# Two layers of hybrid attention on one core: where the steps of the layer normalisation stand among the matrix products

## The reference

```python
for l in range(DEPTH):
    need_ctx = l < DEPTH - 1
    shift, scale, gate = jnp.split(cond @ w_ada[l] + b_ada[l], 3, axis=-1)
    h = x * (1.0 + scale[:, None]) + shift[:, None]
    ...
    x = layer_norm(ALPHA * x + gate[:, None] * y, ln_g[l], ln_b[l])
    if need_ctx:
        cx = layer_norm(ALPHA * cx + gate_c * yc, ln_g[l], ln_b[l])
return x
```

## Time and profile before

| | |
|---|---|
| median of three runs | 1734.81 us |
| the profiled execution, own time | 1734.62 us |
| its span, first to last instruction | 1732.7 us |
| TensorE busy | 94% of the span |
| VectorE busy | 39% |
| ScalarE busy | 32% |
| mean granted TensorE clock | 0.976 of full |
| layer 0's chunk 3 out products end, layer 1's begin | about 973 us |
| layer 1's chunk 2 out products begin | about 1647 us |

### The profile page before, as it was taken

How to read it: one execution, slowest core, us unless ns; L and a number is a source line. 1 busy time by engine, 2 the same in 40 slices (tenths; PEclk the granted TensorE clock), 3 DMA queues, 4 the chain that set the end, 5 groups by cost and what they waited for, 6 DMA issues and landing times.

```text
span 1732.7 us, 25988 instructions
## 1 busy us (share of the span) xinstructions
PE 1624.4 (94%) x10106; PEld 1028.6 (59%) x10106; DVE 671.8 (39%) x1529; ACT 549.1 (32%) x1256; POOL 36.8 (2%) x108
## 2 busy tenths in 40 slices
PE   6999999899999999889999899999899799999996
PEld 4666866556565556544747665675564355555484
DVE  2123444413323214321255624244445265554165
ACT  0232242323323224432022332124214365554023
POOL 0000000000000000000000000000000011111000
PEclk9999999899999999999999998999999899999997
DMA  9100021112123113000545411000001000001353
GB/s 382 55 25 25 1 98 62 61 61 105 43 73 122 50 37 123 25 13 28 183 144 164 161 49 49 13 25 26 13 1 49 25 13 1 25 14 43 107 174 115
DMA packets 41144, 120.63 MB, mean 70 GB/s; under 512 B 4288, under 2 KB 14784, under 8 KB 39744
## 3 DMA queue, kind: packets, MB, share of 16 engines
q1 hardware_dynamic: 41024, 118.97, 19.6%
HBM read 109.52 MB, written 9.44 MB: 69 GB/s over the span
## 4 chain that ended last, share of the span: by engine, by line
PE 72%; issue 16%; DVE 6%; ACT 3%; DMA 1%; POOL 0%; SPq 0%; DVEq 0%; ACTq 0%; POOLq 0%
PE proj L986 22%; PE mixed L986 12%; PE scores L986 5%; PE proj L970 4%; PE mixed L970 3%; PE mixed L1106 3%; PE turned L1092 3%; PE scores L1204 2%; PE scores L1072 2%; PE scores L1232 2%; PE scores L1075 1%; ACT vstage L1669 1%; PE turned L1243 1%; PE mixed L931 1%; ACT yT L1669 1%
## 5 line engine op out<-in xcount | busy, mean ns | idle before, releaser
L986 PE MATMUL proj<-hT,weights 128*128 128x512 f32 (+1 forms) x1280 | 519.5, 552 | 10.3 <-DVE yT L1354 3.6
L986 PEld LDWEIGHTS proj<-hT,weights 128*128 128x128 f32 x1280 | 237.3, 194 | 219.3 <-issue 208.6
L986 PE MATMUL mixed<-hT,weights 128*128 128x512 f32 (+1 forms) x336 | 143.5, 571 | 0.8 <-ACT pair L1669 0.8
L986 PE MATMUL mixed<-yT,weights 128*128 128x256 f32 (+1 forms) x432 | 122.7, 442 | 0.0
L1669 ACT ACTIVATE work<-work,stat 128x640 f32<-128x640 f32 (+8 forms) x144 | 108.8, 755 | 42.6 <-DVE stat L1413 38.8
L1512 DVE SCALAR_TENSOR_TENSOR work<-work,turned 128x128 f32<-128x128 f32 (+1 forms) x152 | 53.0, 349 | 141.5 <-PE turned L1243 138.3
L1669 ACT ACTIVATE work<-turned 128x512 f32<-128x512 f32 (+2 forms) x136 | 72.7, 535 | 109.4 <-PE turned L1088 98.5
L1092 PEld LDWEIGHTS turned<-consts,work 128*128 128x128 f32 (+4 forms) x656 | 75.4, 140 | 53.4 <-issue 34.1
L1092 PE MATMUL turned<-consts,work 128*128 128x128 f32 (+4 forms) x656 | 100.4, 281 | 7.0 <-ACT work L1669 7.0
L986 PEld LDWEIGHTS mixed<-yT,weights 128*128 128x128 f32 x432 | 82.1, 190 | 38.9 <-issue 31.1
L986 PEld LDWEIGHTS mixed<-hT,weights 128*128 128x128 f32 x336 | 62.6, 191 | 63.4 <-issue 61.5
(11 more groups left out here) (249 smaller groups left out, 2124.3 us busy)
## 6 DMA issues: line engine op xcount, KB each, us to landing
weights<-in_weights SPq DMA_DIRECT2D x138, 512.0 KB, 3.6
tables<-in_bias SPq DMA_DIRECT2D x8, 1281.0 KB, 7.1
hT<-in_xT SPq DMA_DIRECT2D x8, 640.0 KB, 16.0
yT<-in_weights SPq DMA_DIRECT2D x8, 512.0 KB, 8.5
work<-in_xT SPq DMA_DIRECT2D x24, 128.0 KB, 3.6
x1T<-yT SPq DMA_DIRECT2D x12, 256.0 KB, 2.2
work<-in_weights SPq DMA_DIRECT2D x4, 512.0 KB, 16.4
pair<-in_weights SPq DMA_DIRECT2D x4, 512.0 KB, 17.4
```

Of the source, the lines that this page charges most:

```text
L986: last = nc.tensor.matmul(PJ[BANK_OF[u]][:, 0:n], weights[:, w % WBUFS, k, :], src[:, k, t0:t0 + n], start=(k == 0), stop=(k == KT - 1))
```

## The change

Two calls of `pace` are changed. The steps, their instructions and the products are the same in number and kind; only the order of the list differs.

```diff
+def last_norms():
+    one, two = norm(1, 1), norm(1, 2)
+    out = [(None, 2.6), (("column_sum", 1, 1), 1.1)] + [(x, 2.05) for x in one[:KT]]
+    out += [(None, 2.9), (one[KT], 0.0), (one[KT + 1], 1.6)] + [(x, 1.1) for x in one[KT + 2:-2]]
+    out += [(("column_sum", 1, 2), 1.0)] + [(x, 1.1) for x in one[-2:]] + [(x, 1.25) for x in two[:KT]]
+    return out + [(None, 2.0), (two[KT], 0.0), (two[KT + 1], 1.6)] + [(x, 0.7) for x in two[KT + 2:]]
...
     s += [("blend",)] + pace(normalise(0, 0), parts[0])
-    s += pace(normalise(0, 1) + normalise(0, 2), parts[1] + parts[2])
...
-    s += pace(normalise(0, 3), ready) + rest
+    s += pace(normalise(0, 1) + normalise(0, 2) + normalise(0, 3), parts[1] + parts[2] + ready) + rest
...
-    s += pace(normalise(1, 1) + normalise(1, 2), parts[0] + parts[1])
+    s += pace(last_norms(), parts[0] + parts[1])
     s += [("column_sum", 1, 3)] + norm(1, 3)
```

## The result

The changed kernel takes 1738.64 us, the median of 18 runs (1734.58 to 1743.08), against 1735.1 us for the kernel before (18 runs, 1732.5 to 1739.89): a ratio of 1.0020, interval 1.0013 to 1.0027. It is **slower by 3.5 us**, 2.3 to 4.7. The forecast was 1734.0 us, no change, with a range up to 1738.5, which the median passes by 0.1 us. The profiled execution took 1738.18 us, span 1736.3. In what follows a ratio is that of the runs of a kernel to runs of the kernel before taken beside them, with its 95% interval.

The account below looks back on a forecast made before the run. TensorE, busy 94% of the span, was taken as the bound, so its stops and half clock count. Layer 0's 2.5 plus layer 1's 0.9 less the tail's 4.2 gave -0.8 us: 1734.0 us, range 1728.5 to 1738.5.

Parts of the forecast that it names:

- The step that failed: Layer 1, chunk 3's residual loads: residual 1 issued at 1681.1, residual 2 landing at 1692.2, TensorE stopping 4.3 us.
- The 4.0 us that I took for a landing: Layer 1: time from a residual load's issue to its landing, taken between 3.4 and 4.7 us from rows before.
- L: End of layer 1's last product: 1710.62 us before, forecast at 1711.5.
- The clock behind that stop: Layer 1, behind the stop at chunk 2's square sum: half clock costs 2.1 us; with 3.3, 1.2 us later still.
- the forecast's 0.9 for layer 1: Layer 1: last product ends 0.9 us later, from a 4.3 us stop at chunk 2's square sum and its half clock.
- The 3.3: Half-clock cost of a start after 4.89 us of idling, half of the eight pairs; used as upper bound.
- Rival B: Layer 1: loads queue behind stores, 7.2 us each, residual 2 landing at 1698.6; 1740.4 us, chance 0.08.
- Layer 0: Chunk 2's stop goes, 7.0 us stop before the 512-wide gate product, half clock costs 2.5 us, bounds 2.1 and 3.3.
- The two things costed at nothing: Layer 0: chunk 3's eight spills, and ScalarE's copies of early gates and q between chunk 2's scalings; no cost.
- The tail: From the last product's end, 13.41 us before: pairs end 9.2 us after it, 4.2 us less, bounds 3.4 and 6.5.
- rival C: Tail keeps full clock, winning 6.5 us in place of 4.2; 1731.7 us, chance 0.14.
- The sum: Layer 0, layer 1 and tail together: 2.5 + 0.9 - 4.2 = -0.8 us, forecasting 1734.0 us by the median.

Follow-up runs that it names:

- The swap: Changed kernel with part 0 of the product of chunk 3, tile 1 put ahead of scale 1 1 5 in the list: ratio 1.0005 against the kernel before.
- the later 12 runs: The changed kernel, unaltered, measured a second time: ratio 1.0014 against the kernel before, 2.4 us slower.
- layer 0's half alone: Changed kernel with layer 1 paced as before, run twice: ratios 1.0025 and 1.0015 against the kernel before.
- the mended kernel: Kernel before with layer 0's early gate products alone moved, layer 1 in the change's order, residual loads two products sooner: 1716.32 us (0.9893), again 1719.56 us (0.9906).

## Why the prediction was wrong

**The step that failed** is in the residual loads of layer 1: "residual 1, issued behind the store of tiles 2 and 3 at 1681.1". In the new list part 0 of that product stands behind `scale 1 1 5`, as the table of the change says, so its load waits for the store of tiles 4 and 5, and this one for scalings that VectorE makes only after residual 0. On the forecast's scale (5.36 us less than the trace after, by where chunk 2's products start) residual 1 left at 1684.8 and not at 1681.1, residual 2 at 1691.0 and not at 1688.2, and residual 2 was there at 1695.0 and not at 1692.2. The 2.8 us pass into the stop unchanged: 7.06 against 4.3. I had followed the list for tiles 1, 3 and 7 and not for tile 5. The 4.0 us that I took for a landing were right on average: VectorE had the three loads 4.4, 3.2 and 4.0 us after their issue. But they would not have held at the place I had for residual 1. The swap puts it there (1681.0 on the forecast's scale), it took 5.2 us, and the stop was 5.42 and not 4.3. So of the 2.8 us the place alone is worth 1.6.

The Trainium skill (DMA: Bandwidth & Descriptors, section Specifications) gives about 358 GB/s from HBM for one core, by which I had estimated L 1 us later. The slot of the earlier trace rows with 418 GB/s lies above that figure, but it holds no store; from 1685 to 1695 us, with stores and loads under way, the same trace moved 361 GB/s on average. So the 418 were no fair rate for such a group, though with landings of 3.9 us on average the sum needs no further term.

**The clock behind that stop** was too small by 0.7 us: square sum and nine quarters took 11.03 us (1709.32 to 1720.35) where 8.2 are due, so 2.8 and not 2.1, inside the bound of 3.3. With 2.8 + 0.7 the forecast's 0.9 for layer 1 becomes 4.4, as measured. The 2.1 itself was misread: behind the stop of 2.34 us the square sum still took 0.70 us, and of the window 1706 to 1708 in the trace of before

```profile
1706.00:1708.00 2.00, 2.00 (x7) 1.66 (x6) 0.00 (x0) 0.89 (x2) 0.00 (x0) 0.59 0.00 0
```

0.59 puts the fall at 1706.36, so half clock lasted 3.4 us and cost 1.7. The 3.3 is 3.1 by the same reading, and the square sum at half clock is 1.22 in the earlier trace rows, not 1.12. Rival B (a longer queue) had the sign and nearly the place, but not the cause: none of these three loads took 7.2 us.

**Layer 0 was right** in its mechanism: square sum of chunk 2 without a wait, stop of 7.0 (7.13), gate product at the old time to 0.1 us, half clock behind it. It cost 2.0 us in four traces and 1.4 in two, where the clock rose 4.1 and 2.7 us behind the gate product's start; I had 2.5, with a lower bound of 2.1 that came from the misread 2.07. The two things costed at nothing cost nothing: the transposes wait the same 3.25 us.

**The tail** gave 6.2 us and not 4.2 against the first trace of before (5.8 against the second), alike in both traces of the changed kernel, so rival C came true there: its stops of 1.09 and 1.56 us did not bring the half clock. In the other five traces with this order the pairs took 5.4 to 5.5 us and the tail 8.8, which is 4.6 less than the first trace of before and 4.3 less than the other old-order ones. The 9.2 that I took lies above both. Which of the two the timed runs had isn't known.

**The sum** with these sizes is 2.0 + 4.4 - 6.2 = 0.2, or 1.8 with the tail of 8.8, each 0.6 less with 1.4 for layer 0. So in the traces of the changed kernel the failed step's 3.5 us in L were for the most part offset by the tail and by layer 0, and the changed steps come to within 1.0 us of the forecast's -0.8. That the tail made good what the loads lost was luck. The 18 runs say 3.5, at least 2.3, the later 12 runs 0.3 to 4.7. The traces of the changed kernel and of the one before, two each, are 2.3 us apart on average (spans 1736.3 and 1735.5 against 1732.7 and 1734.5), of which 2.2 are in the stretch between the row transposes and chunk 2's products.

**A second step failed with it**: a term that the prediction has at nothing: that behind the row transposes all goes as before, shifted. The traces alone can't show what the change does there, but the granted clock of the timed runs points the same way as their time. It is 0.9767 on average in the 30 runs of the changed kernel, 0.9764 in the 19 with layer 0's half alone and 0.9782 in 84 runs of the kernel before (95% intervals of the two differences: 0.0010 to 0.0021 and 0.0011 to 0.0025). That makes 5.5 and 6.4 us more at half clock. The traces of the changed kernel and of the one before place none of it at the changed steps: at those of layer 0 the half clock lasts 6.8 us in all four, and from chunk 2's products in layer 1 on it lasts 14.9 us in the changed kernel against 19.5 and 16.5 before. In the untouched stretch a trace with 34.1 us at half clock took 5.8 us longer than one with 20.5, 0.42 us for each, so by my estimate 5.5 more are worth 2.3 us. So the sign of the loss is shown, and the share of the changed steps in it: 0.2 us with the tail of their own traces, up to 1.8 with the other. That the rest is half clock in untouched parts fits all of this, but no run tests it, and by what way the change brings it about stays open.

## What to carry to other kernels

A queue that walks one list in order couples every load to every store ahead of it, and a store waits for compute that may itself wait for the load before: when a step with a store in it is moved, write down for each load of the stretch what stands directly ahead of it, each one and not a sample. Filling a stop pays only if the work that fills it was not covering another wait: here the products moved up had lain over the next chunk's scaling, and the stop came back at full length, in a place that leaves the clock down for the critical product. And when two profiles differ by a few us in code that didn't change, take a second profile of the old kernel before explaining it, and compare the mean granted clock of the timed runs.

## What the runs showed of the hardware

- TensorE's clock fell or stayed full in the same place of the same program from one execution to the next. One stretch of 570 to 576 us of identical code varied by 6 us, in the mended kernel by 5.8 between its two executions. The four traces whose clock fell 0.9 to 1.1 us ahead of its first matmul agreed in it to 0.2 us. One trace so bears a term of 1 to 2 us only where the stretch around it is compared by itself.
- Stops of 1.09 and 1.56 us with 0.70 us of work between left the clock full in the two traces of the changed kernel; with the same stops the pairs behind took 3.9 us there and 5.4 to 5.5 in the others. Behind a stop of 4.89 us they took 6.3 to 6.7 in all seven traces with the old order.
- A residual load of 128 KB directly behind a store of 512 KB was there after 3.2, 3.6 and 4.0 us, behind a store and weights after 4.2 and 4.4, and behind a store and weights with another such group still under way after 5.2 (one load). Leaving 3.8 us sooner, that one was there 1.8 us sooner.
